# Forty-eight prompt attention steps placed between the groups of the sample attention

## The reference, cut to what matters

```python
# prompt: 12 heads, 4 blocks of 128 queries, keys of the prompt itself
sc = jnp.einsum('bqhd,bkhd->bhqk', qb, k).astype(F32) * scale
sc = sc + cb[..., :, None] - cum[..., None, :]          # cum: running sum of log forget gates
sc = jnp.where(kpos[None, :] <= qpos[:, None], sc, -jnp.inf)
p = jax.nn.softmax(sc, axis=-1)
return jnp.einsum('bhqk,bkhd->bqhd', p.astype(v.dtype), v)

# sample: 8 sequences, 8 new queries each, 4096 past rows gathered page by page, and the new rows
s_past = jnp.einsum('bqhd,bkhd->bhqk', q, k_past) * scale + g[..., :, None] + suffix[..., None, :]
s_new = jnp.einsum('bqhd,bkhd->bhqk', q, k) * scale + g[..., :, None] - g[..., None, :]
p = jax.nn.softmax(jnp.concatenate([s_past, s_new], axis=-1), axis=-1)
```

## Time and profile before

| | us |
|---|---|
| median of three runs | 2286.21 |
| profiled execution | 2289.08 |
| its span | 2287.2 |
| input projection, first to last product | 48.7 to 185.3 |
| prompt attention on PE, first to last | 240.6 to 356 |
| first cache page issued | 358.75 |
| first group scored, from | 374.10 |
| last page weighed | 931.2 |
| output projection begins | 935.93 |

### The profile page before, as it was taken

How to read it: one execution, slowest core, us unless ns; L and a number is a source line. 1 busy time by engine, 2 the same in 40 slices (tenths; PEclk the granted TensorE clock), 3 DMA queues, 4 the chain that set the end, 5 groups by cost and what they waited for, 6 DMA issues and landing times.

```text
span 2287.2 us, 40891 instructions
## 1 busy us (share of the span) xinstructions
PE 1981.6 (87%) x16723; PEld 1487.8 (65%) x16723; DVE 1064.5 (47%) x1915; ACT 354.2 (15%) x817; POOL 197.5 (9%) x266
## 2 busy tenths in 40 slices
PE   6999885666766666889999999999997899999996
PEld 4777663444444444667777777677775677777774
DVE  5331855565665565453334444232456533344443
ACT  2002451111111111112221000111011022210002
POOL 1000500000000000100001222100001100002221
PEclk9999997888788898999999999999898999999998
DMA  4221106999999999312222222222111222222221
GB/s 162 74 74 38 63 2 225 340 373 357 372 367 355 357 384 367 119 37 74 74 74 90 93 76 74 74 74 74 39 32 56 74 74 74 74 74 74 74 74 42
DMA packets 127990, 320.42 MB, mean 140 GB/s; under 512 B 10236, under 2 KB 10514, under 8 KB 127678
## 3 DMA queue, kind: packets, MB, share of 16 engines
q1 hardware_dynamic: 124258, 304.67, 36.4%
q0 software_dynamic: 3296, 12.98, 1.7%
q10 hardware_dynamic: 252, 0.16, 0.0%
HBM read 309.20 MB, written 8.55 MB: 139 GB/s over the span
## 4 chain that ended last, share of the span: by engine, by line
PE 76%; DVE 8%; DMA 6%; issue 5%; SPq 4%; ACT 1%; ACTq 0%; DVEq 0%
PE ps L847 49%; PE ps L1047 7%; DMA work<-in_cache_k 5%; DVE work L1898 3%; PE ps L1161 3%; PE ps L1162 3%; SPq L540 2%; PE ps L769 1%; PE ps L770 1%; PE ps L996 1%; SPq L545 1%; PE ps L798 1%; PE ps L799 1%; SPq L528 1%; PE ps L1069 1%
## 5 line engine op out<-in xcount | busy, mean ns | idle before, releaser
L1898 DVE STREAM_TRANSPOSE work<-work 128x768 f32<-128x768 f32 x256 | 245.2, 971 | 160.9 <-DMA work<-in_cache_k 160.1
L847 PE MATMUL ps<-xn,wring 128*128 128x288 f32 x1104 | 295.5, 411 | 20.0 <-DVE xn L1617 15.7
L847 PE MATMUL ps<-work 128*128 128x288 f32 x1152 | 296.5, 411 | 12.4 <-DVE work L1664 7.8
L847 PEld LDWEIGHTS ps<-work 128*128 128x128 f32 x1152 | 221.7, 193 | 75.6 <-issue 13.7
L847 PEld LDWEIGHTS ps<-xn,wring 128*128 128x128 f32 x1104 | 212.4, 193 | 80.7 <-issue 20.0
L847 PE MATMUL ps<-big,wring 128*128 128x288 f32 x944 | 251.4, 410 | 7.6 <-DVE big L2172 7.6
L1047 PE MATMUL ps<-work,big 32*32 32x256 f32 x6144 | 165.4, 471 | 92.2 <-DVE work L1898 61.6
L847 PEld LDWEIGHTS ps<-big,wring 128*128 128x128 f32 x944 | 181.0, 192 | 58.7 <-DVE big L2172 8.5
L1047 PEld LDWEIGHTS ps<-work,big 32*32 32x32 f32 x6144 | 113.9, 115 | 136.4 <-DVE work L1898 74.3
L1691 DVE TENSOR_TENSOR work<-ps,work 128x288 f32<-128x288 f32 x72 | 33.0, 458 | 320.1 <-PE ps L847 320.1
L702 POOL TENSOR_TENSOR h<-h,xn 128x288 f32<-128x288 f32 x96 | 106.1, 1108 | 812.4 <-DVE xn L1698 697.6
(11 more groups left out here) (348 smaller groups left out, 2345.2 us busy)
## 6 DMA issues: line engine op xcount, KB each, us to landing
work<-in_cache_k SPq DMA_DIRECT2D x256, 384.0 KB, 5.9
big<-in_cache_v SPq DMA_DIRECT2D x256, 384.0 KB, 7.5
wring<-in_w_up SPq DMA_DIRECT2D x16, 2048.0 KB, 7.6
wring<-in_w_down SPq DMA_DIRECT2D x16, 2048.0 KB, 7.8
wring<-in_w_in_odd SPq DMA_DIRECT2D x6, 2048.0 KB, 8.1
wring<-in_w_in_even SPq DMA_DIRECT2D x5, 2048.0 KB, 9.1
wring<-in_w_out_even SPq DMA_DIRECT2D x2, 2048.0 KB, 8.4
wring<-in_w_out_odd SPq DMA_DIRECT2D x2, 2048.0 KB, 7.8
```

The costliest lines, as they stand in the source:

```text
L847: last = mm(bank, w[:, k, :], x[:, k, :], start=k == 0 and not onto, stop=k == 3, skip_group_check=onto)
L1898: nc.vector.transpose(x, x).then_inc(sem("k_turned"), 1)
```

## The change

The 48 prompt steps no longer run ahead of the cache loads. Steps 2g and 2g + 1 run inside group g of the sample attention, so groups 0 to 23 score two steps each, and the turning and weighing of the last step fall into group 24. What follows from that:

- The prompt attention has one score bank (0), one bank for turned probabilities (1) and one for the output (2, shared with the new rows of the samples). Step n is scored only after step n - 1 has been through the exponential.
- `qz`, `kz` and the copies into them are gone. ACT scales q once, in place, in the input projection. The scores read q and k where they were projected, and the gates come by a product of their own (`ident[:, hd:hd+1]` times `gates`), as wide as the scores.
- SP starts the key pages once the suffix sums are copied out. The first value page waits until k is stored. PE's groups wait until v is stored.
- The value ring, `kstage` and the probabilities lie in `wring`. The two units of the output projection go to `big` and are loaded behind the last key page, ahead of the last eight value pages.
- The pooling mixer's POOL work starts after the first pair of the input projection; its products run ahead of the groups.
- The new rows of a sequence are scored one group earlier (`GS - 3`), turned and weighed in the next.

The diff, cut to its core:

```diff
@@ SP
-            unit("out0", 0)
-            unit("out0", 1)
             sp.wait_ge(sem("ptab_in"), 16)
-            sp.wait_ge(sem("ngate_ready"), 1)
-            sp.wait_ge(sem("qz_zeroed"), 1)
-            sp.wait_ge(sem("kz_zeroed"), 1)
-            for hd in range(H):
-                ...
-                sp.dma_start(kz[hd % 2][r:r + 1, :], ngate[hd:hd + 1, :]).then_inc(sem(f"gates_in_{hd % 2}"), 16)
-            sp.wait_ge(sem("fox_prompt_done"), H)
+            wait_emptied(sp, FIRST["sfx"] + 6)
...
             def v_page(n, page):
+                if n == 0:
+                    sp.wait_ge(sem("k_stored"), 80)
+                    sp.wait_ge(sem("new_keys_turned"), 1)
...
+            sp.wait_ge(sem("fox_prompt_done"), H)
+            unit("out0", 0)
+            unit("out0", 1)
             for n in range(NB * PAGES - GP, NB * PAGES, 4):
@@ PE
+            pe.wait_ge(sem("v_stored"), 32)
+            gates = rstd[:, 0:SEQ]
             def score(n):
                 hd, i = n // NT, n % NT
...
-                if n >= 4:
-                    pe.wait_ge(sem("probs_made"), n - 3)
-                mm(bank[:, 0:w], qz[:, hd % 2, i * P:w], kz[hd % 2][:, 0:w], start=True, stop=False)
-                mm(bank[:, i * P:w], ident, cst("mask"), start=False, stop=True).then_inc(sem("scores_made"), 1)
+                if n:
+                    pe.wait_ge(sem("probs_made"), n)
+                mm(ps[:, 0, 0:w], big[r, EV_Q + hd // 2, i * P:w], big[r, EV_K + hd // 2, 0:w], start=True, stop=False)
+                mm(ps[:, 0, 0:w], ident[:, hd:hd + 1].broadcast_to([P, P]), gates[:, 0:w], start=False, stop=False)
+                mm(ps[:, 0, i * P:w], ident, cst("mask"), start=False, stop=True).then_inc(sem("scores_made"), 1)
...
+            def prompt_step(n):
+                if n >= NT + 1 and (n - 1) % NT == 0 and n <= NSTEP + 1:
+                    weigh((n - 1) // NT - 1)
+                if 1 <= n <= NSTEP:
+                    turn(n - 1)
                 if n < NSTEP:
                     score(n)
...
             for g in range(NG):
                 score_group(g)
                 if g:
                     for p in range(GP // 2, GP):
                         weigh_page(g - 1, p)
+                prompt_step(2 * g)
                 turn_probs(g)
                 for p in range(GP // 2):
                     weigh_page(g, p)
+                prompt_step(2 * g + 1)
@@ ACT
             for g in range(NG):
+                if 1 <= 2 * g - 1 < NSTEP:
+                    exp_prompt(2 * g - 1)
+                if 0 <= 2 * g - 2 < NSTEP:
+                    take_turned(2 * g - 2)
                 exp_group(g)
+                if 1 <= 2 * g - 1 < NSTEP:
+                    take_turned(2 * g - 1)
                 take_probs(g)
+                if 2 * g < NSTEP:
+                    exp_prompt(2 * g)
@@ DVE
                 turn_pages(g + 1, range(0, 3))
+                if 1 <= 2 * g - 1 < NSTEP:
+                    divisors(2 * g - 1)
                 shift_group(g)
                 if g:
                     add_out(g - 1)
+                if 2 * g < NSTEP:
+                    maximum(2 * g)
+                if g % 2 == 1 and g >= 3 and g // 2 - 1 < H:
+                    head_out(g // 2 - 1)
+                turn_pages(g + 1, range(3, 4))
                 if g + 1 < NG:
                     turn_bias(g + 1)
+                turn_pages(g + 1, range(4, 5))
+                if 2 * g < NSTEP:
+                    divisors(2 * g)
+                turn_pages(g + 1, range(5, 8))
+                if 2 * g + 1 < NSTEP:
+                    maximum(2 * g + 1)
```

More of the change, by code:

```diff
@@ L313, in hybrid_step @@
+        ep = [work[:, W1 + 2 * EXT * n:W1 + 2 * EXT * (n + 1)].rearrange("p (a t) -> p a t", a=2) for n in range(2)]
+        es = [work[:, W1 + 4 * EXT + 368 * n:W1 + 4 * EXT + 368 * (n + 1)].rearrange("p (a b t) -> p a b t", a=2, b=NB)
+              for n in range(2)]
         lg = work[:, 0:3072].rearrange("p (a s h) -> p a s h", a=2, h=H)
-        kstage = work[:, 0:3840].rearrange("p (t n) -> p t n", t=NT + 1)
         lT = xnf[:, 0:3072].rearrange("p (a h g) -> p a h g", a=2, h=H)
@@ L484, in unit @@
                 u = UFIRST[stage] + j
-                if u >= 2:
+                if u >= 2 and stage != "out0":
                     for name, n, per in WEIGHTS:
@@ L816, in _ @@
             pe.wait_ge(sem("params_ready"), 1)
+            pe.wait_ge(sem("hist_in"), 16)
+            for a in range(2):
+                s = slot("hist", a)
+                open_block(FIRST["hist"] + a)
+                tr(ps[:, 2 * s, 0:NB * HIST], hstage[:, a * P:(a + 1) * P], ident[0:NB * HIST, 0:NB * HIST])\
+                    .then_inc(block_in, 1)
             s = slot("logf")
@@ L894, in _ @@
             pe.wait_ge(sem("c11_out_in"), c11_before(last_in + 1, "in"))
+            s = slot("hist_out")
+            for a in range(2):
+                tr(ps[0:NB * HIST, 2 * s + a, 0:P], hcopy[:, a, :], ident)
+                last = tr(ps[0:HIST, 2 * s + a, P:2 * P], hcopy_p[:, a, :], ident)
+            last.then_inc(block_in, 1)
             pe.wait_ge(sem("lg_in"), 32)
@@ L1112, in _ @@
                 score_group(g)
+                if g % GS == GS - 2 and new < NB:
+                    turn_new(new)
                 if g:
@@ L1756, in _ @@
             first_weight_sums("in", 0)
+            for a in range(2):
+                s = drained("hist", a)
+                cp(es[0][:, a, :, 0:HIST], ps[:, 2 * s, 0:NB * HIST].rearrange("p (b t) -> p b t", b=NB))\
+                    .then_inc(out_of["vector"], 1)
             norm(0, PROW["norm_mix"], 0)
@@ L1770, in _ @@
             act_sum(0, "T4")
-            pairs(pairs_of("in", 0))
+            pairs(pairs_of("in", 0), under_in)
             dve.wait_ge(sem("c11_out_in"), c11_before(pairs_of("in", 0)[-1] + 1, "in"))
+            nc.vector.memset(rstd[:, :], 0.0).then_inc(sem("gates_zeroed"), 1)
+            s = drained("hist_out", 0)
+            for a in range(2):
+                cp(hout[:, a * P:(a + 1) * P], ps[0:NB * HIST, 2 * s + a, 0:P])
+                last = cp(hout_p[:, a * P:(a + 1) * P], ps[0:HIST, 2 * s + a, P:2 * P])
+            last.then_inc(out_of["vector"], 1)
+            wait_emptied(dve, FIRST["hist_out"] + 1)
+            dve.sem_inc(sem("hist_out_ready"), 1)
             dve.wait_ge(sem("log1p_ready"), 1)
```

386 lines of the change are left out of this document (159 added, 227 removed).

## The result

The changed kernel took 2257.9 us (median of four runs, 2255.59 to 2264.43); the kernel before took 2287.31 beside it. The ratio is 0.9874 [0.9849, 0.99]: 1.3% faster. Forecast were 2203 and a range of 2170 to 2244. The direction was right, the gain about a third of the forecast (30 of 84 us). The profiled execution has a span of 2256.5 us, 30.7 less than before.

What follows compares the result with a forecast made beforehand. Prompt attention with idle DMA stood ahead of sample groups paced by transfers at 17.47 us, PE having little slack. -113.7 (start) + 27 (longer periods) + 3 (weights) = -84 us, giving 2203 us, range 2170 to 2244.

Steps and rivals of the forecast that it cites:

- The start: First scores of the sample groups at 260.4 us instead of 374.10, limited by v's store: -113.7 us (-119 to -108).
- The wait for turned pages: PE's wait for DVE's turned key pages, 1.85 us a group before; prompt steps ahead of the scores would fill it.
- the other loop (through `divisors`): DVE's `divisors` ahead of the last three key pages lengthens their loop from 8.8 to 10 us, hidden by PE's path.
- rival 3: Prompt steps wait across ACT and DVE in single banks and fill no gap: 22.7 us a group, 2300 us; chance 0.06.
- rival 4: Something ahead of v's store holds PE, so groups start at 300 instead of 260 us: 2243 us; chance 0.03.
- the period of a group with two prompt steps: Groups 0 to 23, from PE's path: 18.6 us instead of 17.47, so +27 us over 24 groups.
- the "issue" stall: Stall of PE within a group's scores that no row explains, taken as 1.65 us a group.
- the share for the clock: Half of the 1.7 us a group that PE's lowered clock costs was left in the period: 0.8 us.
- own work and steps at full clock: PE's work in a group: 9.8 us of its own plus 5.2 us for two prompt steps.
- ACT's copy: PE's wait between turning and weighing for the copy of turned probabilities, which no prompt step can fill: 1.0 us a group.
- Rival 2: The clock stays where it is, for prompt steps too: 20.2 us a group, 2242 us; chance 0.19.
- the term of the weights: Output projection's weights, loaded ahead of the last eight value pages, delay the last of these: +3 us (0 to 11.6).

Runs made afterwards that it cites:

- quarter_after: The changed kernel with only a quarter of each page's columns loaded behind the first 12 key and 8 value pages, all instructions kept: 2144.97 us, ratio 0.9362.
- quarter_before: The kernel before with only a quarter of each page's columns loaded behind the first 12 key and 8 value pages: 2226.51 us, ratio 0.9737.
- mid_split: The changed kernel with the second step's score amid the next group's scores, and the first step turned ahead of the group's probabilities, scored behind: 2230.11 us.
- mid_mask: The changed kernel with the second step's score amid the next group's scores, and the mask added on DVE instead of by a product: 2233.22 us.
- mid_split_mask: The changed kernel with second step's score amid next group's scores, first step turned ahead of group's probabilities and scored behind, mask added on DVE: 2233.26 us.
- mid: The changed kernel with only the score of a group's second prompt step moved into the middle of the next group's scores: 2234.44 us, ratio 0.9771.
- burst: The changed kernel with a group's whole second prompt step moved into the middle of the next group's scores: 2256.13 us, ratio 0.9852.

## Why the prediction was right and wrong

**The frame was right.** The start was forecast at -113.7 and came at -111.1; every step of the chain through v's store is in the trace within 2 us (240.4 and 249 forecast, 238.22 and 249.97 measured), and the new-row products to the first scores took 13.0 us instead of 11.35. (The forecast's slow end, -108, doesn't follow from its own 251 us for v's landing, which gives -112.) The wait for turned pages went, the other loop (through `divisors`) didn't bite, and no wait for a single bank shows: rival 3 did not happen, nor rival 4. PE's busy share is 81%, though (357.98 of 440), where over 85% was the mark, and the DMA share is 0.86 and 0.92 where 0.92 and 0.97 were.

**The step that failed is the period of a group with two prompt steps**, 18.6 forecast, 20.3 measured; over 20 was its own sign of being wrong. Within it the terms that failed are the "issue" stall and the share for the clock:

| term, us a group | forecast | measured | from |
|---|---|---|---|
| own work and steps at full clock | 9.8 + 5.2 = 15.0 | 15.04 | quarter_after |
| clock and hand-overs | 0.8 + 0.15 | 1.5 | 357.98 / 21.7 - 15.04 |
| ACT's copy | 1.0 | 1.13 | 24.5 / 21.7 |
| "issue" stalls | 1.65 | 2.64 | (45.1 + 8.7 + 3.4) / 21.7 |
| sum | 18.6 | 20.3 | |

The work was right to a tenth. One us is the stalls. Nearly half of that was in the profile before and left out: the forecast took only the row at the scores (47.1), while the same view has one more:

```profile
PE ps L1069 <- issue: 12.9, 6, 3.2
```

That is 0.45 us a group at the weighing of pages. The other half is growth: the forecast took the stall as a constant of the scores, with nothing known of its cause. A group now has more program to load (671 records in place of 622), the traffic stayed high (DMA share 0.86), and 0.16 of it is "issue" ahead of the prompt steps (3.4 / 21.7). How much each adds isn't shown. That the stall is gone at a quarter of the traffic is shown by quarter_after and quarter_before. Half a us more is the clock: it rose from 0.85 to 0.93, but the stalls remained, and the clock fell only at them; in quarter_after, where they are gone, it was granted in full from 290 to 650 us (1.00, so 2.4 GHz). The forecast left half of the clock's cost without a reason from a row. The rule of the Trainium skill that the prediction named ("TensorE: Matmul & The Clock Gate", section "HAM oscillation — how this bites in real kernels") has the direction right in both. That it would take the clock's term out altogether was the prediction's use of it, and that didn't come: the prompt steps filled two gaps a group and left the stalls.

**The transfers did not cover the rest.** With PE's path above 17.5 us the transfers hide none of it, and each period counts 24 times. (The removals gave back only half to two thirds, because other waits came in their place.) 1.7 us of error in a group are 39 of the 53 us by which the forecast of -84 was off.

**Rival 2 gave the period (20.2 us) by another mechanism.** It had the clock stay at 0.85 for everything. The clock did rise; the stalls took its place, so that the period fits is luck. Its time, 2242, was 16 us short even so, mostly because of the end.

**The end** was forecast at +3 and came at +14. 4.8 of it is the tail, the term of the weights, near enough. 9.4 is the last seven groups, which no term had; their clock was 0.81 (the row of 756 to 886), and in other kernels with the same loads the same seven periods were up to 1.2 us shorter.

**The best version** is mid_split: 2230.11 us, 0.9708 [0.9674, 0.9742] of the kernel before, by the ratios two thirds of the way from the changed kernel (0.9874) to the one without any prompt steps (0.9619). Its margin over mid_mask and mid_split_mask is inside their intervals; mid's, [0.9742, 0.98], only touches its own, and the two were timed on different chips, with medians 4 us apart.

## What to carry to other kernels

When work is put beside a transfer-bound loop, add up the engine's whole path through one period at both clocks with every wait of that engine that the view lists, "issue" at every line included, and expect nothing to be hidden once the sum passes the period of the transfers. A stall that nothing in the dependencies explains is worth one run with the traffic cut to a quarter, which tells whether it needs the traffic, and one count: whether the stalls stand at the same place of every 256 records of the engine. And where several waits stand close behind each other in a loop, taking one away shows the next; here such repairs gave about half of what they took off PE, and didn't add.

## What the runs showed of the hardware

Dense runs of small products can outrun the loading of their own program. Here 448 records in about 5 us, with page loads at 0.86 of the DMA engines, stalled PE for up to 3.5 us at a time and 2.1 us a group; at a DMA share of 0.35 the same instructions cost it 0.25 us. All 18 stalls over 1.5 us stand at the same place of a block of 256 records, and PE goes on 1.2 to 1.5 us after a 16 KB packet of program has landed. That it was the program which came late is an inference from these counts; what makes the packet begin late is open. A few wide products (128 columns and more) in the middle of such a run took the stall away without taking any traffic away: burst has no "issue" wait at the scores at all, and mid 1.0 us a group in place of 2.1.

Between 300 and 730 us the granted clock fell from 1.00 to 0.50 only at such stalls: all twelve falls begin in one or within 1.6 us of its end. In quarter_after, without the stalls, it was 1.00 from 290 to 650 us.
